# Six pieces of the second feed-forward layer: the down projection as seven block products of Strassen's identity in place of eight

## The reference, cut to what matters

```python
def _sq_relu_mlp(h, w1, w2):
    return jnp.square(jax.nn.relu(h @ w1)) @ w2
...
x = _layernorm(DN_ALPHA * x + g2 * _sq_relu_mlp(x * (1.0 + s2) + sh2, ffn_w1[i], ffn_w2[i]),
               ln2_g[i], ln2_b[i])
```

## Time and profile before

| | |
|---|---|
| median of 3 runs | 2003.33 us (2003.31 to 2003.67) |
| profiled execution, span | 2001.8 us |
| PE busy in the span | 1991.0 us, 99% |
| DVE, ACT, POOL busy | 1197.8, 602.0, 483.5 us |
| one piece of `ffn1` | 43.52 us |

### The profile page before, as it was taken

The page is one execution under the profiler, slowest core; times in us unless marked ns, Lnnn a source line. Parts: engine busy times, 40 slices in busy tenths (PEclk is TensorE's granted clock), DMA queues, the critical chain, the costliest instruction groups (busy, mean ns, idle before and its releaser), DMA issues.

```text
span 2001.8 us, 26691 instructions
## 1 busy us (share of the span) xinstructions
PE 1991.0 (99%) x9765; PEld 1710.1 (85%) x9765; DVE 1197.8 (60%) x1683; ACT 602.0 (30%) x861; POOL 483.5 (24%) x366
## 2 busy tenths in 40 slices
PE   9999999999999999999999999999999999999998
PEld 6889889889988998898888888888888888888887
DVE  4756678787655755566764553644553586544547
ACT  3423122244212221222424223223323343332223
POOL 0300321334331135233350010020020036322323
PEclk9999999999999999999999999999999999999999
DMA  9623334323433432344322132122222232333332
GB/s 342 232 64 82 119 114 130 105 85 116 142 95 110 126 110 89 113 129 138 105 69 63 52 98 67 53 90 63 74 64 79 64 105 74 102 98 95 115 105 74
DMA packets 76420, 207.56 MB, mean 104 GB/s; under 512 B 13232, under 2 KB 26160, under 8 KB 76208
## 3 DMA queue, kind: packets, MB, share of 16 engines
q1 hardware_dynamic: 74512, 202.57, 33.0%
q10 hardware_dynamic: 1824, 3.85, 0.6%
HBM read 204.26 MB, written 2.12 MB: 103 GB/s over the span
## 4 chain that ended last, share of the span: by engine, by line
PE 97%; DMA 1%; DVE 0%; POOL 0%; issue 0%; ACT 0%; SPq 0%; POOLq 0%; ACTq 0%; DVEq 0%
PE bank L760 24%; PE bank L762 24%; PE bank L761 24%; PE bank L798 7%; PE bank L800 7%; PE bank L799 7%; PE bank L1064 1%; PE bank L1113 1%; PE bank L976 1%; DMA mod<-mod_units_d 0%; PE bank L948 0%; PE bank L998 0%; PE bank L999 0%; PE bank L996 0%; PE bank L1199 0%; DMA raw<-w_units_d 0%
## 5 line engine op out<-in xcount | busy, mean ns | idle before, releaser
L1683 DVE TENSOR_TENSOR w_lo<-raw,w_hi 128x1024 fp32r<-128x1024 f32 x234 | 312.6, 1336 | 366.5 <-ACT w_hi L1341 366.2
L1341 ACT ACTIVATE w_hi<-raw 128x1024 fp32r<-128x1024 f32 x234 | 246.8, 1055 | 661.2 <-PE bank L762 451.8
L2356 POOL TENSOR_TENSOR res_lat<-res_lat,gy 128x512 f32<-128x512 f32 x160 | 221.6, 1420 | 697.8 <-DVE gy L1792 589.5
L760 PE MATMUL bank<-hT_hi,w_hi 128*128 128x384 f32 (+2 forms) x1088 | 379.5, 349 | 0.0
L762 PE MATMUL bank<-hT_hi,w_lo 128*128 128x384 f32 (+2 forms) x1088 | 377.9, 347 | 0.0
L761 PE MATMUL bank<-hT_lo,w_hi 128*128 128x384 f32 (+2 forms) x1088 | 377.9, 347 | 0.0
L798 PE MATMUL bank<-w_hi,hT_hi 128*128 128x512 f32 x592 | 230.6, 389 | 0.0
L799 PE MATMUL bank<-w_lo,hT_hi 128*128 128x512 f32 x592 | 230.3, 389 | 0.0
L800 PE MATMUL bank<-w_hi,hT_lo 128*128 128x512 f32 x592 | 230.3, 389 | 0.0
L760 PEld LDWEIGHTS bank<-hT_hi,w_hi 128*128 128x128 f32 x1088 | 204.5, 188 | 13.5 <-DVE w_lo L1683 0.7
L761 PEld LDWEIGHTS bank<-hT_lo,w_hi 128*128 128x128 f32 x1088 | 204.5, 188 | 12.8 <-issue 0.2
(11 more groups left out here) (275 smaller groups left out, 3010.4 us busy)
## 6 DMA issues: line engine op xcount, KB each, us to landing
raw<-w_units_d SPq DMA_DIRECT2D x255, 512.0 KB, 3.6
mod1a<-mod_units_d SPq DMA_DIRECT2D x32, 384.0 KB, 3.9
mod1b<-mod_units_d SPq DMA_DIRECT2D x32, 384.0 KB, 4.2
bv<-mod_units_d SPq DMA_DIRECT2D x16, 512.0 KB, 3.9
mod<-mod_units_d SPq DMA_DIRECT2D x14, 512.0 KB, 7.7
mod<-mod_units_d SPq DMA_DIRECT2D x19, 256.0 KB, 6.1
vtok<-mod_units_d SPq DMA_DIRECT2D x8, 512.0 KB, 3.9
lnbc<-ln_d SPq DMA_DIRECT2D x8, 512.0 KB, 5.1
```

Of the source, the lines that this page charges most:

```text
L760: nc.tensor.matmul(out, s_hi, m_hi, start=first, stop=False)
L1341: nc.scalar.activation(halves_of(phase, k, i)[0], raw[:, s, :], ACT.Copy).then_inc(hi_done, 1)
L1683: tt(lo, raw[:, s, :], f32(hi), ALU.subtract).then_inc(lo_done, 1)
L2356: gt(r, r, gy[:, e % 2, :], ALU.add).then_inc(res_added, 1)
```

## The change

The six pieces of `ffn1` compute their down projection as a product of 2x2 blocks. The activations A are cut in two halves of 256 tokens and two of 256 hidden features, the weights B in 256 features by 512 columns, so that B's blocks are the four loaded units. Each block product has 2 token tiles, 2 chunks and 3 matmuls: 12 matmuls, seven of them instead of eight.

- **POOL** forms four wide sums of weight blocks (T3, T1, T2, T4, in `wsum`) and four narrow ones of activation blocks (S3, S1, S2, S4, in `sraw`). It no longer adds to the residual in these pieces.
- **ACT and DVE** split four `w1` units and seven weight operands (three blocks as loaded, four sums), and seven activation operands of narrow size. In the list `PRODUCTS` each product has its pair of banks; products 2, 4 and 3 go on in the banks of 1, 7 and 5.
- **DVE** adds each product's two banks to one of five accumulators that stay in SBUF over all six pieces (`accumulate`, 14 narrow instructions a piece, in place of 8 drains). PE may reuse a pair of banks only after that.
- After the last of the six pieces DVE makes the outputs with six narrow additions (`combine`), and POOL multiplies the eight parts by the gate and adds them to the residual (16 narrow instructions, "the fold"); `ffn1z`'s results wait for it. POOL clears the accumulators first, and `ln_shift` moves behind the first piece's sums.
- The loop over the six pieces is written out on every engine.

```diff
+PRODUCTS = [(1, 0, True), (7, 4, True), (2, 0, False), (4, 4, False), (5, 2, True), (6, 0, True), (3, 2, False)]
+NPROD = len(PRODUCTS)
+_STRASSEN = [(f"up{c}.0", (6, 7, 2, 3)[c], "A") for c in range(CH)]
+_STRASSEN += [(f"q{q}.{t}", b + t, "D") for q, b, _ in PRODUCTS for t in range(2)]
...
+                for x in range(4):
+                    sp.wait_ge(lo_done, split + x + 1)
+                    load(at + CH + UNIT_OF[x], x)
+                sp.wait_ge(lo_done, split + CH + 1)
+                sp.wait_ge(t_sum, 4 * p + T1 + 1)
+                load(at + 8, B11)
+                load(at + 9, B12)
+                sp.wait_ge(lo_done, split + CH + 3)
+                sp.wait_ge(t_sum, 4 * p + T4 + 1)
+                load(at + 11, B21)
+                sp.wait_ge(lo_done, split + CH + NPROD)
+                load(at + 10, B22)
+            for k in range(CH):
+                sp.wait_ge(lo_done, before("splits", "ffn1z") + k + 1)
+                load(BASE["ffn1z"]["units"] + CH + k, k)
...
+                for n, (q, b, opens) in enumerate(PRODUCTS):
+                    pe.wait_ge(lo_done, before("splits", "ffn1", p) + CH + n + 1)
+                    pe.wait_ge(stage_lo, count("stage", "ffn1", p, n))
...
+                    for t in range(2):
+                        free("ffn1", p, f"q{q}.{t}")
+                        tt = slice(t * P, (t + 1) * P)
+                        out = bank[b + t][:, :]
+                        for kk in range(2):
+                            w = slice(kk * 512, (kk + 1) * 512)
+                            nc.tensor.matmul(out, a_hi[:, kk, tt], hi[:, w], start=opens and kk == 0, stop=False,
+                                             skip_group_check=True)
+                            nc.tensor.matmul(out, a_hi[:, kk, tt], lo[:, w], start=False, stop=False, skip_group_check=True)
+                            last = nc.tensor.matmul(out, a_lo[:, kk, tt], hi[:, w], start=False, stop=kk == 1,
+                                                    skip_group_check=True)
+                        last.then_inc(pe_step, 1)
...
             ffn1("ffn1a", 0, True)
-            with nc.tensor.Fori(0, PIECES_F - 2) as p:
-                ffn1("ffn1", p)
+            for p in range(PIECES_F - 2):
+                strassen(p)
...
+            INTO = {1: (SUM16, ALU.add, 6, 1), 7: (Z57, ALU.subtract, 5, 1), 2: (C11, ALU.add, 2, 1), 4: (C21, ALU.add, 4, 1),
+                    5: (Z57, ALU.add, 7, 0), 6: (SUM16, ALU.add, 1, 0), 3: (C12, ALU.add, 3, 1)}
+
...
+                def accumulate(q):
+                    a, op, last, back = INTO[q]
...
+                    for t in range(2):
+                        dve.wait_ge(pe_step, step_of("ffn1", p, f"q{q}.{t}"))
+                        if p >= back:
+                            dve.wait_ge(dve_drain, drained("ffn1", p - back, f"q{last}.{t}")[1])
+                        else:
+                            dve.wait_ge(acc_zero, 1)
+                        tt(acc[:, a, t, :], acc[:, a, t, :], bank[b + t][:, :], op).then_inc(dve_drain, 1)
...
+                block_lo(p, 2)
+                block_lo(p, 3)
+                square(0)
+                block_lo(p, 4)
+                square(1)
+                block_lo(p, 5)
+                operand_lo(0)
+                operand_lo(1)
+                square(2)
+                block_lo(p, 6)
+                square(3)
+                block_lo(p, 7)
+                operand_lo(2)
+                operand_lo(3)
+                accumulate(1)
+                operand_lo(4)
+                block_lo(p, 8)
+                accumulate(7)
+                operand_lo(5)
+                block_lo(p, 9)
+                accumulate(2)
+                operand_lo(6)
+                block_lo(p, 10)
+                accumulate(4)
+                accumulate(5)
+                block_lo(p + 1, 0)
+                accumulate(6)
+                block_lo(p + 1, 1)
+                accumulate(3)
+
+            def combine():
+                for a, op, t in ((C12, ALU.subtract, 0), (C12, ALU.subtract, 1), (C21, ALU.add, 0), (Z57, ALU.subtract, 0),
+                                 (C21, ALU.add, 1), (Z57, ALU.subtract, 1)):
+                    dve.wait_ge(dve_drain, drained("ffn1", PIECES_F - 3, "q3.1")[1])
+                    tt(acc[:, a, t, :], acc[:, a, t, :], acc[:, SUM16, t, :], op).then_inc(combined, 1)
...
+                    dve.wait_ge(folded, 2 * t + (1 if at.stop <= 512 else 2))
...
@@ -2463,10 +2706,58 @@
             ln_scale("ln1a", 2, lnbc1, LAT)
             pool.wait_ge(res_mul, 2 * (BASE_RES["ln1b"] - TILES0))
             add("ffn1a", 0, LAT)
...
+            def weight_sum(p, x):
...
+                a, b = ((raw[:, B12, :], raw[:, B22, :]), (raw[:, B11, :], raw[:, B12, :]),
+                        (wsum[:, T1, :], raw[:, B22, :]), (wsum[:, T2, :], raw[:, B21, :]))[x]
+                gt(out, a, b, ALU.add).then_inc(t_sum, 1)
...
+                pool.wait_ge(stage_full, count("full", "ffn1", p, 1 if x == S3 else 3))
+                if p:
+                    pool.wait_ge(stage_lo, count("stage", "ffn1", p - 1, {S3: 1, S1: 4, S2: 5, S4: 6}[x]))
...
+                a, b, op = ((a11, a21, ALU.subtract), (a21, a22, ALU.subtract), (s_of[S1], a11, ALU.subtract),
+                            (a12, s_of[S2], ALU.add))[x]
+                gt(s_of[x], a, b, op).then_inc(s_sum, 1)
...
+            nc.gpsimd.memset(acc[:, :, :, :], 0.0).then_inc(acc_zero, 1)
+            for p in range(PIECES_F - 2):
+                if p == 0:
+                    pool.wait_ge(pe_step, step_of("ffn1a", 0, "up3.0"))
+                weight_sum(p, T3)
+                weight_sum(p, T1)
+                weight_sum(p, T2)
+                operand_sum(p, S3)
+                weight_sum(p, T4)
+                for x in (S1, S2, S4):
+                    operand_sum(p, x)
+                if p == 0:
+                    ln_shift(before("add", "ffn1"), lnbc1, LAT)
             pool.wait_ge(res_base, BASE_RES["ln1b"])
-            with nc.gpsimd.Fori(0, PIECES_F - 2) as p:
-                add("ffn1", p, LAT)
+            for n, (t, half, a, row, done) in enumerate([(0, 0, 0, 0, 0), (0, 1, 4, 0, 1), (1, 0, 0, 1, 1), (1, 1, 4, 1, 2),
+                                                         (2, 0, 3, 0, 3), (2, 1, 2, 0, 4), (3, 0, 3, 1, 5), (3, 1, 2, 1, 6)]):
+                c = slice(half * 512, (half + 1) * 512)
+                pool.wait_ge(dve_drain, drained("ffn1", PIECES_F - 3, "q3.1")[1])
+                if done:
+                    pool.wait_ge(combined, done)
+                part = acc[:, a, row, :]
+                gt(part, part, gate_lat[:, c], ALU.mult).then_inc(fold_mul, 1)
+                pool.wait_ge(fold_mul, n + 1)
+                gt(res(t)[:, c], res(t)[:, c], part, ALU.add).then_inc(folded, 1)
```

More of the change, by code:

```diff
@@ L203 @@
     PER[_n].update(_k)
+    PER[_n].setdefault("splits", PER[_n]["units"])
 BASE = {}
@@ L246, in implied @@
 def implied(phase, label):
-    if phase.startswith("ffn0") and label in ("up0.0", "up0.1"):
+    if phase.startswith("ffn0") and label in ("up0.0", "up0.1") or phase == "ffn1" and label in ("up2.0", "up3.0"):
         return False
@@ L729, in _, with load @@
             load_gate(3, 1)
-            at += 2
-            weights_from(at, TOTAL["units"] - 16 - at)
-            sp.wait_ge(res_base, BASE_RES["ln1a"] + LAT)
-            load_lnbc(lnbc1, 6)
-            weights_from(TOTAL["units"] - 16, 16)
+            for u in range(at + 2, at + 10):
+                weights(u)
+            def load(u, slot):
+                sp.dma_start(raw[:, slot, :], w_units[u]).then_inc(w_in[slot], 16)
+            for p in range(PIECES_F - 2):
+                at, split = BASE["ffn1"]["units"] + 8 * p, before("splits", "ffn1", p)
+                if p == 2:
+                    sp.wait_ge(res_base, BASE_RES["ln1a"] + LAT)
+                    load_lnbc(lnbc1, 6)
+                for x in range(4):
[13 more added lines that the diff above has]
+                load(BASE["ffn1z"]["units"] + CH + k, k)
             def store(t, c):
@@ L1285, in part @@
                             seen.add(k)
-                            pe.wait_ge(lo_done, before("units", "ffn1z") + (k + 1))
+                            pe.wait_ge(lo_done, before("splits", "ffn1z") + (k + 1))
                         hi, lo = halves_of("ffn1z", k)
@@ L2329, in _ @@
             ffn("ffn1a", 0, 1, TOKL, act_hi1, act_lo1, LAT)
-            with nc.vector.Fori(0, PIECES_F - 2) as p:
-                ffn("ffn1", p, 1, TOKL, act_hi1, act_lo1, LAT)
+            for p in range(PIECES_F - 2):
+                strassen(p)
+            combine()
             ffn("ffn1z", 0, 1, TOKL, act_hi1, act_lo1, LAT)
```

176 lines of the change are left out of this document (156 added, 20 removed).

## The result

The changed kernel takes 2027.69 us (median of four runs, 2025.76 to 2029.24), the kernel before 2003.32 beside it (2003.05 to 2003.67). The ratio is 1.012, with a 95% interval of 1.0108 to 1.0133: slower, as forecast, but by 24.4 us and not by 14.7.

The account below looks back on a forecast made before the run. PE was taken as the bound, busy 1991.0 of 2001.8 us. Terms -16.3 + 12.6 + 3 + 15.5 = +14.8 gave a span of 2016.6, and with the median 1.5 above, 2018 us; range 1999 to 2029.

Parts of the forecast that it names:

- turns at SBUF: DVE and POOL instructions with two SBUF inputs wait for each other: about 1.1 us per narrow one, wide sums 2.4.
- 16.3 us of matmuls, nothing for the written-out program: Six pieces: 72 matmuls removed at 0.2267 us save 16.3 us; writing out the loop costs nothing.
- a turn may be given up halfway: Alternative reading of a trace row: a piece some 1 us shorter, and the total +9 us.
- The steady piece: Timeline of one ffn1 piece: first accumulation at 28.9 us, PE ready at 27.2, so PE waits 1.7.
- Then a square, a wide split, a square and a wide split: 24.8: Steady piece: four DVE instructions after S3's low half is split at 21.3 us, ending at 24.8.
- 2.1 us a piece, 12.6 for six: Six pieces: PE's 1.7 us wait plus restart and a short wait at product 4, 2.1 us each, 12.6 in all.
- First piece "I take 3": First piece: clearing the accumulators and ln_shift beside DVE's splits cost 3 us, bounds 0 and 9.
- Last piece 15.5: Last piece: combine ahead and the fold beside DVE's splits make PE wait 14.5 us, 15.5 with restarts and the fourth chunk's split.
- The 37.65 us: Last piece: DVE's work and turns before the product opening the second half of columns; PE is there at 23.1.
- The port costs nothing: Rival for the whole change: sharing the port costs nothing on the path, 1987 us; chance 0.12.
- DVE goes first: Rival: POOL yields to DVE, so sums come just in time and products wait about 1.3 us a piece; 1997 us; chance 0.09.
- DVE paces all pieces: Rival: DVE's queue with its turns exceeds 40.8 us and delay carries over between the six pieces; 2031 us; chance 0.13.

Follow-up runs that it names:

- e1: Changed kernel with the fold's 16 GpSimd instructions in the last piece working on 8 columns in place of 512; 2013.67 us.
- e2: Changed kernel with GpSimd's eight sums a piece made 4 to 8 columns wide from the second piece on, order and waits kept; 2009.91 us.
- e8: Changed kernel with GpSimd's eight two-input sums a piece replaced by one-input scalings at full width, order and waits kept; 2006.77 us.
- e3: Changed kernel with GpSimd's sums computed but not read; ScalarE and VectorE split a constant gate row in their place; 2028.72 us.
- e4: Changed kernel with the eight sums a piece moved from GpSimd to VectorE and ln_shift back in front of POOL's work; 2018.26 us.

## Why the prediction was right in kind and short in size

The changed kernel was forecast slower, by turns at SBUF, and that is what the runs show: e1, e2 and e8 take the turns away in three ways, and each time the matching part of the loss goes (e8 nearly takes them away: 206.71 us and not 204.00), while e3 keeps the turns and keeps 16.7 of 20.3 us of the loss. Point by point:

- **16.3 us of matmuls, nothing for the written-out program**: right. e2's five pieces take 204.00 us, 180 matmuls each at 0.2267.
- **Turns, at 1.13 us for a narrow one and whole wide sums**: right in mechanism. The lengths I gave, a narrow pair at 1.73 each and a wide sum at 2.4, came out as 1.73 (3.46 for two) and 2.40. The reading of the earlier trace rows, that a turn may be given up halfway, was wrong for the sums: those rows were of a `TENSOR_SCALAR` with one input, and their split began 1.3 us behind its start; e8 shows that this form holds splits at its start alone, and the changed kernel that a sum holds them to its end. The estimate made from the Trainium skill ("GPSIMD Engine Reference", section 3.1, 4497 ns for 2048 elements) was 2.25 us for the wide sum; the trace has 2.40.
- **The steady piece**: T3 at 6.0 (forecast 6.2), S3's end at 17.4 (17.8), T4's at 20.2 (20.7), then the first accumulation done at 29.7 (28.9). The step that failed is "Then a square, a wide split, a square and a wide split: 24.8". S1 starts at 1894.10, as soon as its squares are there, and the second wide split begins 0.18 us later and stands behind it: 2.20 us instead of 1.15, so that the splits are done at 25.7 and not at 24.8. PE waited 2.5 us here, 2.6 on average, and not 1.7.
- **"2.1 us a piece, 12.6 for six"** is the term that was mis-sized: five pieces lost 20.3 us over 204.0, 4.1 each. 2.7 of that is the wait with its restart, where 2.1 with a short wait at product 4 had been put; of the other 1.4 about 1.0 (24 matmuls, 0.2 each, over five pieces) is the lower clock behind the wait, which the sum didn't have at all. The forecast had 12.6 us for six pieces at one rate, the five alone took 20.3.
- **First piece "I take 3"**: 6.7 us over 40.8, where 2.1 and 3 were forecast; within the bounds. PE has three waits, of 1.7, 2.2 and 2.0 us, at products 2, 4 and 3. The first ended at 1718.42, before `ln_shift` began (1718.79), so it is that of every piece. In front of the other two `ln_shift` held the splits for products 5 to 3 as said, and behind these stood the accumulations that PE waited for.
- **Last piece 15.5**: 15.9 measured (60.75 against 44.87). The 37.65 us at which PE would get the split for the second half of columns were 37.3 (the piece begins at 1961.1, the matmul at 1998.36), in three parts where they were forecast. It is e1 that shows it to be the fold. That the sum is so close is partly luck: the waits were 12.7 us where 14.5 were forecast, and 1.6 us of lower clock (8 matmuls), which I had not counted, made up for most of it.
- **The rivals.** *The port costs nothing* fell with the result. *DVE goes first* fell: a DVE instruction that comes during a sum waits to its end, as the earlier trace rows had it. *DVE paces all pieces* named a time, 2031, that came nearer than mine, but not the mechanism: nothing is carried from piece to piece (DVE stands idle for 1.7 to 2.6 us before the first square of each of the five pieces, waiting for ACT's ReLU; the ReLUs of `up0` follow at 45.07, 43.92, 44.93, 43.77 and 46.60 us, and the long ones are those with slow matmuls), and e4 gave DVE 7 us more work a piece and got faster. 2027.7 came of the forecast's mechanism with longer waits and one more price.

## What to carry to other kernels

When work is moved to an idle engine, ask what it reads: a two-input addition on GpSimd can hold up a VectorE instruction with two SBUF inputs for its whole length (2.4 us here), twice what VectorE needs to do it itself (1.2). VectorE's accumulations with one input in PSUM weren't held. Put the instruction that PE will wait for ahead of what isn't needed yet, and put background work where the busy engine waits anyway; the same instructions in other places made 2003.8 into 1998.7 here. And put a wait of PE down at more than its length: behind those of 2.5 us here the matmuls often ran at half the clock, which cost 1.0 to 2.6 us more each time.
